# The modulation sums of the second sequence on GpSimd, those of the first on VectorE

## The reference

```
for i in range(DEPTH):                                   # DEPTH = 2
    mod = jax.nn.silu(c) @ w_mod[i] + b_mod[i]           # w_mod[i]: 1024 x 6144
    sh1, sc1, g1, sh2, sc2, g2 = jnp.split(mod, 6, axis=-1)
    h = modulate(rmsnorm(x, norm1_g[i]), sh1, sc1)
    mix = even_mixer(h, ...) if i % 2 == 0 else odd_mixer(h, ...)
    x = x + g1[:, None, :] * mix
    h = modulate(rmsnorm(x, norm2_g[i]), sh2, sc2)
    x = x + g2[:, None, :] * swiglu(h, ffn_w_gu[i], ffn_w_down[i])
return rmsnorm(x, final_g)
```

## Time and profile before

| | |
|---|---|
| median of 3 runs | 2128.09 us (2118.55 to 2129.23) |
| the profiled execution | 2124.51 us |
| its span | 2122.4 us |
| PE busy | 2017.7 us (95%) |
| DVE busy | 992.6 us (47%) |
| ACT busy | 601.7 us (28%) |
| Pool busy | 74.3 us (4%) |

### The profile page before, as it was taken

One profiled execution on the slowest core, in us unless ns is written; L12 is line 12 of the kernel. 1 busy time (PEld: TensorE's weight loads), 2 busy tenths in 40 slices (PEclk: granted clock), 3 DMA queues, 4 the chain that ended last, 5 costly groups with the idle time before them and its releaser, 6 DMA issues.

```text
span 2122.4 us, 28746 instructions
## 1 busy us (share of the span) xinstructions
PE 2017.7 (95%) x12081; PEld 1742.5 (82%) x12081; DVE 992.6 (47%) x1875; ACT 601.7 (28%) x1101; POOL 74.3 (4%) x121
## 2 busy tenths in 40 slices
PE   7879999988899999999998999998989999999998
PEld 2768888767788888888887788888878888888887
DVE  1877425684766665652235334544452222222224
ACT  3235224652321112211223333334232211211213
POOL 2010000000011101100000000000000000000000
PEclk9889999999899999999998999999989999999999
DMA  7343112012344444432223201021212222222212
GB/s 282 120 150 108 41 41 80 21 31 60 99 142 138 136 122 139 142 96 60 65 62 104 60 20 41 21 99 49 61 50 60 60 70 60 64 66 60 62 56 82
DMA packets 210249, 174.16 MB, mean 82 GB/s; under 512 B 10320, under 2 KB 196792, under 8 KB 208584
## 3 DMA queue, kind: packets, MB, share of 16 engines
q1 hardware_dynamic: 197536, 117.67, 18.5%
q0 software_dynamic: 12288, 48.35, 7.1%
q10 hardware_dynamic: 296, 6.29, 0.7%
HBM read 162.85 MB, written 9.44 MB: 81 GB/s over the span
## 4 chain that ended last, share of the span: by engine, by line
PE 87%; DVE 6%; ACT 4%; issue 2%; DMA 1%; POOL 0%; ACTq 0%; DVEq 0%; POOLq 0%
PE bank L824 60%; PE bank L790 9%; PE bank L842 4%; PE bank L1096 2%; PE bank L747 1%; PE bank L765 1%; DMA early_raw<-in_w_mod_dram 1%; ACT w_hi L1221 1%; DVE early_acc L1620 1%; DVE w_lo L1601 1%; PE bank L1018 1%; PE bank L908 1%; PE bank L1041 1%; PE bank L966 1%; PE bank L1068 1%
## 5 line engine op out<-in xcount | busy, mean ns | idle before, releaser
L824 PE MATMUL bank<-h_hi,w_hi 128*128 128x256 f32 x1600 | 409.4, 338 | 0.1
L824 PE MATMUL bank<-h_lo,w_hi 128*128 128x256 f32 x1600 | 407.5, 336 | 0.0
L824 PE MATMUL bank<-h_hi,w_lo 128*128 128x256 f32 x1600 | 407.3, 336 | 0.0
L1601 DVE TENSOR_TENSOR w_lo<-raw,w_hi 128x1024 fp32r<-128x1024 f32 (+4 forms) x195 | 239.0, 1230 | 340.2 <-ACT w_hi L1221 340.1
L824 PEld LDWEIGHTS bank<-h_hi,w_lo 128*128 128x128 f32 x1600 | 301.3, 188 | 33.6
L824 PEld LDWEIGHTS bank<-h_lo,w_hi 128*128 128x128 f32 x1600 | 301.4, 188 | 33.2
L824 PEld LDWEIGHTS bank<-h_hi,w_hi 128*128 128x128 f32 x1600 | 299.4, 188 | 34.2 <-issue 1.9
L1221 ACT ACTIVATE w_hi<-raw 128x1024 fp32r<-128x1024 f32 (+4 forms) x196 | 205.6, 1053 | 226.3 <-DMA raw<-in_ffn_w_down_dram 129.1
L790 PE MATMUL bank<-w_hi,h_hi 128*128 128x256 f32 x672 | 214.8, 320 | 18.1 <-DVE w_lo L1601 17.7
L790 PE MATMUL bank<-w_lo,h_hi 128*128 128x256 f32 x672 | 195.8, 291 | 0.0
L790 PE MATMUL bank<-w_hi,h_lo 128*128 128x256 f32 x672 | 195.6, 291 | 0.0
(11 more groups left out here) (274 smaller groups left out, 2251.7 us busy)
## 6 DMA issues: line engine op xcount, KB each, us to landing
raw<-in_ffn_w_gu_dram SPq DMA_DIRECT2D x176, 256.0 KB, 3.3
late_raw<-in_w_mod_dram POOLq DMA_DIRECT2D x56, 512.0 KB, 4.3
raw<-in_ffn_w_down_dram SPq DMA_DIRECT2D x64, 256.0 KB, 3.3
early_raw<-in_w_mod_dram POOLq DMA_DIRECT2D x24, 512.0 KB, 4.4
wide<-in_w_mod_dram SPq DMA_DIRECT2D x8, 1024.0 KB, 18.7
raw<-in_odd_w_in_dram SPq DMA_DIRECT2D x16, 512.0 KB, 4.4
raw<-in_even_w_in_dram SPq DMA_DIRECT2D x24, 256.0 KB, 5.0
x_kept<-x ACTq DMA_DIRECT2D x2, 3072.0 KB, 10.3
```

The lines of the kernel that those rows point to most:

```text
L824: last = mm(pair(u.pair)[s], wk[a], seq(operand(o, k), s), start=(k == 0 and n == 0), stop=(k == u.ks - 1 and n == 2))
L1601: v.tensor_tensor(lo, r, hi.bitcast(F32), ALU.subtract).then_inc(unit_split, 1)
```

## The change

The sums of the first sequence stay on DVE. Those of the second are made by Pool, in the loop that issues the loads. [...] The loop of the loads calls it for the part before, ahead of the next load:

```diff
+            def modulate_second(m):
+                b, part = MOD_ORDER[m]
+                pool.wait_ge(mod_loaded[m % 2], 16 * (m // 2 + 1))
+                for kk in range(MOD_KS):
+                    k = part * MOD_KS + kk
+                    acc, c = mod_acc(b)[:, 1, :], c_cols[:, k, 1:2]
+                    chain[0] += 1
+                    if k == 0:
+                        if b >= 2:
+                            pool.wait_ge(mod_full, KD + b)
+                        ins = nc.gpsimd.tensor_scalar(acc, mod_raw(m)[:, kk, :], c, None, ALU.mult)
+                    else:
+                        pool.wait_ge(acc_step[1], chain[0] - 1)
+                        term = (early_term if m < EARLY else late_term)
+                        terms[0] += 1
+                        nc.gpsimd.tensor_scalar(term[:], mod_raw(m)[:, kk, :], c, None, ALU.mult).then_inc(term_ready, 1)
+                        pool.wait_ge(term_ready, terms[0])
+                        ins = nc.gpsimd.tensor_tensor(acc, term[:], acc, ALU.add)
+                    ins.then_inc(acc_step[1], 1)
+
             def mod_loads(first, stop):
                 for m in range(first, stop):
+                    if m > first:
+                        modulate_second(m - 1)
                     b, part = MOD_ORDER[m]
                     l, c = MOD_BLOCKS[b]
                     if m >= 2:
...
                     pool.dma_start(mod_raw(m)[:], src).then_inc(mod_loaded[m % 2], 16)
+                modulate_second(stop - 1)
...
-                    for s in range(2):
-                        acc, c = mod_acc(b)[:, s, :], c_cols[:, k, s:s + 1]
-                        last_of[s] += 1
...
+                    acc, c = mod_acc(b)[:, 0, :], c_cols[:, k, 0:1]
+                    chain[0] += 1
...
+                        dve.wait_ge(acc_step[0], chain[0] - 1)
+                        ins = v.scalar_tensor_tensor(acc, mod_raw(m)[:, kk, :], c, acc, ALU.mult, ALU.add)
+                    ins.then_inc(acc_step[0], 1)
```

More of the change, by code:

```diff
@@ L159, in build @@
         late_acc = [at(f"late_acc{b}", Z + (68 + 4 * b) * KB, [P, 2, MOD_BLOCK]) for b in range(2)]
+        early_term = at("early_term", Z + 6 * KB, [P, MOD_BLOCK])
+        late_term = at("late_term", Z + 86 * KB, [P, MOD_BLOCK])
         ident = own("ident", [P, P])
@@ L285, in build @@
         row_taken = sem("row_taken")
+        term_ready = sem("term_ready")
         hi_ready = sem("hi_ready")
@@ L699, in _ @@
             pool.dma_start(gk_w[B_RANK:2 * B_RANK, 1, :], w["even_gk_w_b"][0]).then_inc(late_loaded, 16)
+            chain, terms = [0], [0]
+            def modulate_second(m):
[17 more added lines that the diff above has]
+                    ins.then_inc(acc_step[1], 1)
             def mod_loads(first, stop):
                 for m in range(first, stop):
+                    if m > first:
+                        modulate_second(m - 1)
                     b, part = MOD_ORDER[m]
@@ L1610, in modulate @@
                     k = part * MOD_KS + kk
-                    for s in range(2):
-                        acc, c = mod_acc(b)[:, s, :], c_cols[:, k, s:s + 1]
-                        last_of[s] += 1
[L1614 to L1623, removed]
+                    acc, c = mod_acc(b)[:, 0, :], c_cols[:, k, 0:1]
+                    chain[0] += 1
+                    if k == 0:
+                        if b >= 2:
+                            dve.wait_ge(mod_full, KD + b)
+                        ins = v.tensor_scalar(acc, mod_raw(m)[:, kk, :], c, None, ALU.mult)
+                    else:
+                        dve.wait_ge(acc_step[0], chain[0] - 1)
+                        ins = v.scalar_tensor_tensor(acc, mod_raw(m)[:, kk, :], c, acc, ALU.mult, ALU.add)
+                    ins.then_inc(acc_step[0], 1)
+            chain = [0]
             def complete(n, l, c0, c1):
```

## The result

The changed kernel takes 2463.61 us at the median (2462.88 to 2466.57), the kernel before 2125.24 us beside it: a ratio of 1.160, 95% interval 1.157 to 1.163, or 338 us. The forecast was 2358 us, 234 us more than before, with a range up to 2440. So the direction and the place were right, and the size was a third too small.

A forecast was written before the change was run, and what follows sets the result against it. PE was taken to bound the late stretch, and early the chain of loads and DVE's sums ran long. Pool's serial cycle of 9.73 us gave shifts of 83.2 + 145.0, plus 6 for clock: 2358 us, range 2245 to 2440.

The forecast's parts named there:

- What bounds the kernel: PE paces the late stretch, hiding DVE; early, DVE's sums can give back at most PE's 12.6 us wait.
- The order matters more than the arithmetic: In Pool's load loop, load m+1 waits for the sums of part m, so the second buffer hides nothing.
- The four terms of the cycle: Per part on Pool, in series: issue 0.56, load 4.3, start 0.04, arithmetic 3.73 us; turns of 1.1 make 9.73.
- the handovers of Pool to itself: Gap between Pool's own consecutive instructions, taken as 0.06 us each.
- 0.56 us of issue: Time from the end of the sums to the start of the next load, in each Pool cycle.
- The load: Each part's load in Pool's cycle, taken as 4.3 us in both stretches.
- Turns: Pool standing back for DVE's two sums on the same tile after each load, 1.1 us a part.
- The sum: Early shift 83.2, late shift 145.0 and clock 6 us: 234 us on 2124.5, giving 2358 us.
- Its own sign: Prediction wrong if Pool's sums and loads overlap, cycle is under 8.1 or over 11 us, or PE's pace is unchanged.
- More than those turns: Rival: DVE's w_lo and other work also block Pool; cycle 10.4 us, 2409 us, range 2390 to 2460, chance 22%.
- Clock: Lower granted clock behind PE's last wait of each stretch costs half of 5.9 us, twice, 6 us.
- What I weighed beside the rows: The skill's measured addition of 2048 fp32 columns, 4497 ns, giving an estimate of 1.12 us for Pool's 512 columns.

The follow-up runs named there:

- experiment 10: Changed kernel with the next load issued ahead of Pool's sums, products by tensor_tensor, and Pool summing only late parts: 2140.82 us, ratio 1.0047.
- experiment 8: Kernel before, all sums on DVE, with a third load buffer for parts 0 to 19: 2119.08 us, ratio 0.9955.
- experiment 1: Changed kernel with the load of part m+1 issued ahead of Pool's sums of part m: 2213.96 us, ratio 1.042.
- experiment 4: Kernel before, no arithmetic on Pool, but each load issued only when the load before it has landed: 2134.07 us, ratio 1.0047.
- experiment 7: Changed kernel with DVE's sums of the first sequence replaced by memsets: 2439.82 us.
- experiment 5: Changed kernel with Pool's products made by tensor_tensor with a repeated column instead of tensor_scalar: 2401.48 us.

## Why the prediction was wrong, by its own steps

- **What bounds the kernel** held for the late stretch: in experiment 10 DVE has half of its late sums less and nothing is gained. For the early one it is shown in part: some 10 us came back with loads in time alone, with all of DVE's sums in place (experiment 8), where the prediction gave at most 12.6 to DVE's sums. The sums taken from DVE are 114 us by the earlier trace rows, but its busy time fell by 38.5 us only (992.6 to 954.1), since what is left takes longer beside Pool.
- **The order matters more than the arithmetic** held: with the load ahead 246 of 338 us come back (experiment 1, where 92 are left), and the wait without arithmetic costs 10 us (experiment 4).
- **The four terms of the cycle.** The step that failed is Pool's product, "I take 0.7", with bounds of 0.61 and 0.87 us from a memset and a cast. It takes 1.56 us. There are two products in every part: 2 x 0.86 = 1.7 us, and 74 cycles of that are 127 us. Both bounds were too low, so the range was too. The addition was 1.27 us for 1.2 (the estimate beside it, 1.12, was further off); the handovers of Pool to itself, 0.07 and 0.09 us, held nearly.
- **0.56 us of issue** isn't there: the load's record starts at 906.01, under the end of the addition at 906.07. In the kernels with the load ahead, where the load itself stands at a semaphore, it is (0.56 in experiment 1). I had taken the row from a handover of DVE to Pool. This error hid 0.6 us of the other.
- **The load**, 4.3 us, held nearly: from its start to the first product 4.33 us in the cycle shown, 4.5 on the mean of all.
- **Turns** held in size, not in make. Pool's late arithmetic is (186.1 + 145.8 + 25.5) / 56 = 6.38 us a part, of the three groups of its timeline, and (112 x 1.56 + 98 x 1.27) / 56 = 5.34 us alone: 1.04 us, against 1.1. But each of DVE's sums costs less than I gave it, since Pool holds DVE up in turn, and `w_lo`, which I left to a rival, costs some 0.9 us where it meets a product. The Trainium skill (SBUF — State Buffer, Who interferes with whom) has the rule that the prediction names. The trace agrees with which pairs meet (experiment 7), and nearly in size: of DVE's first sum 0.67 us are left when the product starts, and 0.55 are added to it. It does not bear out that the one which starts second waits (39 and 16 of 55 in experiment 5; the product at 737.11 in experiment 7).
- **The sum** with the measured cycle: 82.6 + 21 x 11.04 + 4.3 + 7 - 213.1 = 112.6 and 567.6 + 53 x 11.07 + 4.3 + 7 - 947.7 = 217.9, with 7 us for the last part; together 331 us, and 338 were measured. So the form of the sum was right. From 9.73 to 11.05 us the product adds 1.72, the addition 0.12 and the load 0.15, the issue takes 0.6 off, and the rest cancels.
- **Its own sign** of being wrong, a cycle over 11 us, came true (11.04 and 11.07). The rival *More than those turns* came near with its upper bound, a cycle of 11.0 us and 2456 us, by luck: it has the product at 0.87 us, the addition at 1.64 and an issue of 0.56, and what it is named for, more turns, was not what failed.
- **Clock**: PE runs at 0.71 and 0.83 of full clock in the stretches. The sum above gives this no cost and comes within 7 us of the measured loss, so it costs little there, if anything; 2.9 us follow behind the last sum, against 3.
- **What I weighed beside the rows** was the addition, not the product. The Trainium skill (GPSIMD Engine Reference, 4.1, Engine selection) calls operations with one input roughly line-rate on GpSimd, where it compares the engine with VectorE. The measured 1.56 us for 512 columns, against 0.48 for DVE's `tensor_scalar` of that size, differs, and the measurement decides.

## What to carry to other kernels

When arithmetic is put on an engine that also issues loads, write out its queue: if an instruction that waits for load m stands ahead of load m+1, the buffers no longer overlap, and a cycle costs the full series. What is lost is the number of cycles times what that series is over the time the stretch had for one, however idle each engine looks; where it is under, as in experiment 4, next to nothing is lost. Move the load ahead of the arithmetic before anything else. Don't price an instruction from another kind on the same engine: a memset and a cast bounded a product from below only, and when most of the sum hangs on it, the upper bound has to come from elsewhere or stay far away. And a hidden engine's work is worth nothing when it is removed, only when it is what the bound waits for.

## What the runs showed of the hardware

- On Pool, 128x512 in fp32: `tensor_scalar` with a scalar per partition 1.56 us, with a constant 1.48, `tensor_tensor` with a repeated column 1.04, of two tiles 1.27. The two that read only one tile by `tensor_scalar` are the slowest.
- Pool's product of 1.56 us takes 2.11 beside DVE's sums and 2.42 beside `w_lo` in the late stretch of the changed kernel, and up to 2.93 in its early one; the other way round DVE's dependent sum takes 1.06 instead of 0.75 us and `w_lo` 1.8 instead of 1.2. With the same starts, either engine can be the one that waits (experiment 5).
- The same 144 matmuls at full granted clock take 25.07 or 25.54 us in one and the same stretch, with no wait in them, in kernels with and without arithmetic on Pool.
